# Weights split in place, and two staging tiles for every bank, in a two-block transformer kernel

## What is computed

```
h = rms_norm(x, norm_mix)
(a_q, a_kc, ..., merge_gate) = split(h @ w_in)
x = x + sum(sigmoid(merge_gate) * (branches @ w_branch)) @ w_out
x = x + square(relu(rms_norm(x, norm_mlp) @ w_mlp_in)) @ w_mlp_out
...
mod = silu(c) @ w_mod[l] + b_mod[l]
u = h @ e_w_in;  x = x + gate * (y @ w_o[l])
```

## Time and profile before

| | |
|---|---|
| median of 3 runs | 3655.73 us |
| the profiled execution | 3658.32 us |
| its span | 3656.5 us |
| mean granted TensorE clock | 0.947 of full speed |
| PE busy | 3305.0 us (90%), 15207 matmuls |
| DVE busy | 1742.6 us (48%) |
| ACT busy | 1489.2 us (41%) |
| low parts, L394 | 986 of mean 1210 ns |
| high parts, L388 | 986 of mean 1044 ns |
| evacuations to staging, L465 | 148 of 128 partitions and 20 of 4 |
| weight loads from SP | median 4.4 to 7.1 us from issue to landing, by matrix |

### The profile page before, as it was taken

How to read it: one execution, slowest core, us unless ns; L and a number is a source line. 1 busy time by engine, 2 the same in 40 slices (tenths; PEclk the granted TensorE clock), 3 DMA queues, 4 the chain that set the end, 5 groups by cost and what they waited for, 6 DMA issues and landing times.

```text
span 3656.5 us, 39374 instructions
## 1 busy us (share of the span) xinstructions
PE 3305.0 (90%) x15207; PEld 2656.6 (73%) x15207; DVE 1742.6 (48%) x2450; ACT 1489.2 (41%) x2230; POOL 230.2 (6%) x351
## 2 busy tenths in 40 slices
PE   5999999799899999999969999999975979787867
PEld 4888888677778788888847877777754868665546
DVE  3445555455565655666553233334333353345534
ACT  3444444333454554545553232333332143243532
POOL 0000000010000000000010000000011000010010
PEclk9999999899899999999979999999986979898978
DMA  7666745465577777877653423223333215544653
GB/s 216 221 215 226 254 127 182 158 213 184 188 251 236 249 250 241 276 237 254 230 157 102 136 76 113 96 97 114 107 134 120 93 55 157 166 156 148 203 176 124
DMA packets 355878, 634.40 MB, mean 173 GB/s; under 512 B 44715, under 2 KB 111944, under 8 KB 352620
## 3 DMA queue, kind: packets, MB, share of 16 engines
q1 hardware_dynamic: 319772, 543.49, 45.8%
q0 software_dynamic: 19936, 69.22, 5.3%
q10 hardware_dynamic: 15984, 19.17, 1.6%
HBM read 583.00 MB, written 55.08 MB: 175 GB/s over the span
## 4 chain that ended last, share of the span: by engine, by line
PE 81%; DVE 6%; ACT 4%; issue 3%; DMA 3%; POOL 1%; ACTq 1%; SPq 0%; DVEq 0%; POOLq 0%
PE acc L413 24%; PE acc L418 21%; PE acc L417 21%; PE acc L987 3%; PE acc L1014 3%; PE acc L415 2%; DVE w_lo L394 2%; PE acc L1002 2%; PE acc L645 1%; ACT w_hi L388 1%; ACT aff L679 1%; PE acc L991 1%; PE acc L971 1%; ACTq L1145 1%; ACT xn L760 0%
## 5 line engine op out<-in xcount | busy, mean ns | idle before, releaser
L413 PE MATMUL acc<-w_hi,a_hi 128*128 128x512 f32 (+4 forms) x3800 | 1509.1, 397 | 65.0 <-issue 24.1
L394 DVE TENSOR_TENSOR w_lo<-raw,w_hi 128x1024 fp32r<-128x1024 f32 (+1 forms) x986 | 1159.8, 1210 | 840.0 <-ACT w_hi L388 822.6
L417 PE MATMUL acc<-w_lo,a_hi 128*128 128x512 f32 (+4 forms) x3800 | 1474.8, 388 | 0.0
L418 PE MATMUL acc<-w_hi,a_lo 128*128 128x512 f32 (+4 forms) x3800 | 1474.2, 388 | 0.0
L388 ACT ACTIVATE w_hi<-raw 128x1024 fp32r<-128x1024 f32 (+1 forms) x986 | 1000.1, 1044 | 892.6 <-PE acc L418 881.6
L413 PEld LDWEIGHTS acc<-w_hi,a_hi 128*128 128x128 f32 x3800 | 720.9, 190 | 230.8 <-DVE w_lo L394 43.1
L418 PEld LDWEIGHTS acc<-w_hi,a_lo 128*128 128x128 f32 x3800 | 720.3, 190 | 146.9
L417 PEld LDWEIGHTS acc<-w_lo,a_hi 128*128 128x128 f32 x3800 | 721.0, 190 | 132.6 <-issue 1.0
L1111 DVE TENSOR_REDUCE at_st<-acc 128x1 f32<-128x256 f32 (+3 forms) x208 | 101.3, 487 | 445.4 <-PE acc L987 302.3
L1044 ACT ACTIVATE pb<-acc,at_st 128x256 f32<-128x256 f32 (+3 forms) x208 | 108.5, 521 | 381.5 <-DVE at_st L1111 358.3
L645 PE MATMUL acc<-ident,xn 128*128 128x128 f32 x336 | 86.7, 426 | 161.4 <-DVE xn L1688 49.0
(11 more groups left out here) (316 smaller groups left out, 1659.5 us busy)
## 6 DMA issues: line engine op xcount, KB each, us to landing
raw<-in_w_mod SPq DMA_DIRECT2D x192, 512.0 KB, 5.2
raw<-in_w_mlp_in SPq DMA_DIRECT2D x128, 512.0 KB, 4.6
raw<-in_w_mlp_out SPq DMA_DIRECT2D x128, 512.0 KB, 5.4
raw<-in_e_w_in SPq DMA_DIRECT2D x104, 512.0 KB, 5.0
raw<-in_w_in SPq DMA_DIRECT2D x96, 512.0 KB, 4.8
raw<-in_w_in SPq DMA_DIRECT2D x88, 472.0 KB, 4.8
raw<-in_w_o SPq DMA_DIRECT2D x64, 512.0 KB, 4.9
raw<-in_o_w_in SPq DMA_DIRECT2D x64, 512.0 KB, 4.4
```

What stands on the lines that cost most here:

```text
L394: nc.vector.tensor_tensor(w_lo[:, n % SPLITS, 0:size], raw[:, n % RAWS, 0:size], w_hi[:, n % SPLITS, 0:size].bitcast(F32), ALU.subtract)\
L413: nc.tensor.matmul(o, s.lhs(0, kt, tt), wh, start=kt == 0, stop=False)
L417: nc.tensor.matmul(o, s.lhs(0, kt, tt), wl, start=False, stop=False)
L418: last = nc.tensor.matmul(o, s.lhs(1, kt, tt), wh, start=False, stop=end)
```

## The change

The low part of a chunk is written over the raw chunk that it comes from: `w_lo` is placed at the address of `raw`, with 8 tiles in place of 4, and DVE's instruction at L394 writes where it reads. A raw tile is therefore in use until PE has done the chunk's last matmul, and SP waits for `w_used` of chunk n - 8 where it waited for `lo_ready` of chunk n - 8. The four tiles of `w_lo` (16 KB in each partition) are gone. In their room every bank gets a second staging tile (8 KB more for the four banks, 2 KB more for bank 4), used in turn by the bank's count of stores `put`; each of the two has a semaphore of its own, so that ACT waits for the bank's store before the last one. `put_by` replaces the waits of the readers of stored results: it waits on both semaphores of a bank.

```diff
--- before.py
+++ after.py
@@ -138,9 +138,9 @@
             return nc.dram_tensor(name, shape, F32, kind="Internal").ap()
 
 
-        raw = sb("raw", [P, RAWS, CH])
+        raw_at = take(4 * RAWS * CH)
+        raw, w_lo = place("raw", [P, RAWS, CH], raw_at), place("w_lo", [P, RAWS, CH], raw_at, F32R)
         w_hi = sb("w_hi", [P, SPLITS, CH], F32R)
-        w_lo = sb("w_lo", [P, SPLITS, CH], F32R)
         act_hi_at, act_lo_at = take(32768), take(32768)
         a_hi = place("a_hi", [P, 8192], act_hi_at, F32R)
         a_lo = place("a_lo", [P, 8192], act_lo_at, F32R)
@@ -148,7 +148,7 @@
         CX_AT = take(16384)
         CX = place("CX", [P, 2, DM], CX_AT)
         MIX = CX
-        stage = sb("stage", [P, 4, G])
+        stage = sb("stage", [P, 8, G])
         ident = sb("ident", [P, P])
         small = sb("small", [P, 64])
         half = sb("half", [P, 2])
@@ -338,8 +338,12 @@
         w_used = sem("w_used")
         acc_done = [sem(f"acc_done{b}") for b in range(3)]
         acc_free = [sem(f"acc_free{b}") for b in range(5)]
-        stored = [sem(f"stored{b}") for b in range(5)]
-        stage_bufs = [stage[:, b, :] for b in range(4)] + [sb("stage_mod", [4, G])[:, :]]
+        stored = [[sem(f"stored{b}_{i}") for i in range(2)] for b in range(5)]
+        stage_mod = sb("stage_mod", [4, 2, G])
+
+        def stage_buf(bank, put):
+            return stage_mod[:, put % 2, :] if bank == 4 else stage[:, 2 * bank + put % 2, :]
+
         nsa_g = sb("nsa_g", [P, 2, 24])
         nsa_ready, nsa_out = sem("nsa_ready"), sem("nsa_out")
         mfr, mfb, mfo = sb("mfr", [P, 4, NM]), sb("mfb", [P, NM]), sb("mfo", [P, 2, NM])
@@ -371,7 +375,7 @@
         def sp_chunk(sp, g, c):
             n = g.no[c]
             if n >= RAWS:
-                sp.wait_ge(lo_ready, n - RAWS + 1)
+                sp.wait_ge(w_used, n - RAWS + 1)
             dst = raw[:, n % RAWS, 0:g.wtiles * g.width].rearrange("p (k n) -> p k n", k=g.wtiles)
             sp.dma_start(dst, g.chunks[c]).then_inc(landed[n % RAWS], 16)
 
@@ -391,7 +395,7 @@
         def split_lo(dve, s, c):
             n, size = s.no[c], s.wtiles * s.width
             dve.wait_ge(hi_ready, n + 1)
-            nc.vector.tensor_tensor(w_lo[:, n % SPLITS, 0:size], raw[:, n % RAWS, 0:size],
+            nc.vector.tensor_tensor(w_lo[:, n % RAWS, 0:size], raw[:, n % RAWS, 0:size],
                                     w_hi[:, n % SPLITS, 0:size].bitcast(F32), ALU.subtract)\
               .then_inc(lo_ready, 1)
 
@@ -408,7 +412,7 @@
                 o = acc[:, bank, 0:s.width]
                 kt = c * s.wtiles + k
                 wh = w_hi[:, n % SPLITS, k * s.width:(k + 1) * s.width]
-                wl = w_lo[:, n % SPLITS, k * s.width:(k + 1) * s.width]
+                wl = w_lo[:, n % RAWS, k * s.width:(k + 1) * s.width]
                 end = kt == len(s.chunks) * s.wtiles - 1
                 nc.tensor.matmul(o, s.lhs(0, kt, tt), wh, start=kt == 0, stop=False)
                 if s.lhs is lhs_mod:
@@ -455,14 +459,14 @@
             for bank, tt in s.tiles:
                 if e["kind"] == "store":
                     wait_done(act, s, bank)
-                    if s.put[bank]:
-                        act.wait_ge(stored[bank], 16 * s.put[bank])
+                    if s.put[bank] >= 2:
+                        act.wait_ge(stored[bank][s.put[bank] % 2], 16 * (s.put[bank] // 2))
                     r = e["rows"]
                     if e.get("gates"):
                         c0 = e["gates"]
                         nc.scalar.activation(nsa_g[:, tt, :], acc[:, bank, c0:c0 + 24], ACT.Tanh, scale=0.5)\
                           .then_inc(nsa_ready, 1)
-                    nc.scalar.activation(stage_bufs[bank][0:r, 0:s.width], acc[0:r, bank, 0:s.width],
+                    nc.scalar.activation(stage_buf(bank, s.put[bank])[0:r, 0:s.width], acc[0:r, bank, 0:s.width],
                                          e["func"], scale=e["scale"]).then_inc(acc_free[bank], 1)
                 elif e["kind"] == "relu2":
                     wait_done(act, s, bank)
@@ -550,8 +554,8 @@
             e = s.evac
             for bank, tt in s.tiles:
                 pool.wait_ge(acc_free[bank], s.fill[bank] + 1)
-                pool.dma_start(e["dst"](tt, s.width), stage_bufs[bank][0:e["rows"], 0:s.width])\
-                    .then_inc(stored[bank], 16)
+                pool.dma_start(e["dst"](tt, s.width), stage_buf(bank, s.put[bank])[0:e["rows"], 0:s.width])\
+                    .then_inc(stored[bank][s.put[bank] % 2], 16)
             if e.get("gates"):
                 pool.wait_ge(nsa_ready, 2)
                 pool.dma_start(AG.rearrange("(t p) n -> p t n", p=P), nsa_g[:, :, :]).then_inc(nsa_out, 16)
@@ -576,18 +580,23 @@
                 elif s.evac["kind"] == "store":
                     pool_store(pool, s)
 
+        def put_by(eng, bank, k):
+
+            for i in range(2):
+                if (k + 1 - i) // 2:
+                    eng.wait_ge(stored[bank][i], 16 * ((k + 1 - i) // 2))
+
         def wait_stored(eng, upto):
 
             for b in range(5):
                 k = stages[upto].upto.get(("put", b), 0)
-                if k:
-                    eng.wait_ge(stored[b], 16 * k)
+                put_by(eng, b, k)
 
         def wait_step(eng, name, i):
 
             s_ = stages[name].steps[i]
             for bank, _ in s_.tiles:
-                eng.wait_ge(stored[bank], 16 * (s_.put[bank] + 1))
+                put_by(eng, bank, s_.put[bank] + 1)
 
         def wait_freed(eng, upto):
```

## The result

| kernel | median us | runs | lowest to highest |
|---|---|---|---|
| before | 3656.95 | 17 | 3649.93 to 3658.91 |
| after | 3664.95 | 17 | 3661.13 to 3670.70 |

The ratio is 1.0024, 95% interval 1.0017 to 1.0032: slower by 0.24%, outside the range of 3649 to 3662 and on the side that had 8%. The profiled execution took 3664.08 us, its span 3662.3, 5.8 more than the span before. Two of all executions, one of e4 (4147 us, granted clock 0.77) and one of the kernel before beside e5 to e8 (4922 us, 0.65), ran at a lower clock than the rest and stand in no median.

What follows compares the result with a forecast made beforehand. The prediction took PE's weight matmuls (PE busy 90%) as the bound. Staging tile -1.1 and small waits +0.2, all else 0, gave -0.9 us: 3657.4 for the profiled execution, 3654.8 against the median, range 3649 to 3662.

Steps and rivals of the forecast that it cites:

- SP's later wait: Weight loads wait for PE's last use, going out up to four chunks later: 0 us, bounds 0 and +3.7.
- What stands behind SP's later wait: Attention pass rows on SP's in-order queue come some 11 us later, but are read 30 or 86 us on: 0.
- opening: Weight loads at 49 to 93 us: shorter queue, chunk 15 still 0.9 us in time; 0, upper bound 2.6.
- compression weights: Loads at 350 to 370 us: 7.5 us to land against a slowest 7.6, just in time; 0, bound +0.2.
- MLP: MLP with modulation steps beside it: 11.0 us left for landing against a slowest 7.3; covered.
- The first rival: Opening starves PE, landings keeping 18.8 us: 3660.9, or 3664.5 with PE at half clock after stalls; chance 7%.
- any pass starts later than its predecessor's end moved: One of the prediction's own tests, over all passes: if seen, the forecast is wrong.
- Second staging tile: ACT's waits for QB and KVB stores go, saving PE 0.45 and 0.65 us: -1.1, bounds 0 and -11.3.
- The second rival: ACT's staging waits in the attention passes are worth all their 11.3 us: 3644.6; chance 5%.
- the third: Staging evacuations stay late, so the change does nothing and only +0.2 stands: 3655.9; chance 4%.
- Low parts in place: DVE's subtraction writing over its input takes no longer: 0, at most 1.9 us on the path either way.
- Small waits: Readers of stores on SP, POOL and ACT wait on two semaphores instead of one: +0.2, bounds 0 and +1.

Runs made afterwards that it cites:

- e4: Kernel before, with SP's rows for the third attention region's first pass held until PE's last use of chunk 879; 3660.40 us.
- e5: Changed kernel, third region's first rows moved after its fifth chunk, loads from chunk 705 held until the modulation vector landed; 3657.48 us.
- e8: Kernel before, with the third region's first rows moved and holds at chunks 705, 815 and 888; 3649.88 us.
- e7: Kernel before, with SP's late wait for PE's matmuls at chunks 704 to 712 only; 3659.26 us.
- e1: Kernel before, with only SP's wait changed, to PE's last use of chunk n - 8; 3668.85 us.
- e9: Changed kernel, with the third region's first rows moved and holds at chunks 215, 705, 815 and 886; 3648.61 us.
- e10: e9 with only the first staging tile of each bank in use; 3650.88 us.
- e11: Kernel before, with SP's late wait at all chunks plus e9's holds and moved rows; 3654.69 us.
- e3: Changed kernel, with the third attention region's first rows and loads issued behind its fifth weight chunk instead of ahead of its first; 3661.25 us.
- e6: e5 with two more holds, at chunk 815 for the second modulation vector and chunk 888 for the low-rank norms' loads; 3654.26 us.

## Why the prediction was wrong

**SP's later wait: 0, bounds 0 and +3.7.** The step that failed is the paragraph "What stands behind SP's later wait". It took the rows at 3139.93, found their first reader 86 us on the earlier trace rows, and wrote "I take 0 for all". The 0 counts only who waits for the moved transfer, not whose transfer it then runs beside. The reader's slack was right: nobody waited for them. But a transfer costs others too. What I had to ask of every moved DMA is which small transfer with a waiter it now runs beside. The cost measured, alone: +3.6 (e4, this place; 3.9 in its step), +2.1 (e7, the MLP's end; 2.7 in its step, and its interval includes 0). With the less certain one at 808 it is 7.6 us of steps in the changed kernel, and the late wait as a whole cost 12 in e1.

The sign was in the rows. The prediction put PE's 27.0 us of waits for low parts at step starts, "and the change leaves that order alone". 14.6 of them are the single wait at 3180.28, for the norms' chain of store, loads and DVE: the one that grew to 19.7.

I also looked for trouble only where the queue was slow in reaching PE: opening, compression weights, MLP. There I was right. In the opening, 54 to 92 us, the loads land after

```profile
DMA to landing us min/median/max: 4.7/10.2/12.4
```

in place of 11.9/16.2/18.8, as I wrote (8 to 13) but for the quickest, and PE needs 102.02 us from the end of chunk 1 to that of chunk 40 in both kernels. The line in the queue was a line, and it got shorter. The first rival named the right side, slower, for the wrong reason: by it PE would have starved there. Its 3664.5 is near the time measured, which proves nothing for it. Nor does the half clock that it takes from the gap at 3247 follow from that gap: in before the granted clock was already 0.50 from 3240 on, in an idle of 9.08 us that ended at 3243.

Of my own tests the nearest was "any pass starts later than its predecessor's end moved"; what it caught is not a pass but the norms ahead of one, at DVE's first multiply.

**Second staging tile: -1.1, bounds 0 and -11.3.** Right in kind and place, half of what came in size: -2.3 in e9 against e10, and -2.2 in the step 885 to 900 of the changed kernel. The evacuation that had waited at 3216.76 no longer waits for a store; PE passes without the gap of the earlier trace rows. At the two places of the sum the changed kernel gains 0.54 (chunk 894, 0.45 forecast) and 0.84 us (chunk 900, 0.65 forecast); the other 0.8 of its 2.2 lies at chunks 886 and 888, ahead of any QB evacuation, and isn't the tile's. In e9 against e10 the gain is spread over chunks 894 to 900. The second rival, the full 11.3, is excluded by the same pair, and so is the third, that it does nothing.

**Low parts in place: 0, bound 1.9 either way.** The instruction's time was right: 1210 ns mean after as before. The term was not, as far as the pair e10 and e11 measures it alone: 3.8 us gained, twice the bound, with no place for it.

**Small waits: +0.2.** No run separates them; too small to be measured.

In sum: -0.9 was forecast and +8.0 came. The later wait had 0 in it where e1 shows +12; the staging tile and the low parts give back about 2 and 3 to 4. 12 less 5 to 6 is 6 to 7 where 8.0 was measured; the rest is within what these medians can tell: they and the traces differ by as much (8.0 between medians, 5.8 between spans).

## What to carry to other kernels

When a change moves bulk loads later, their readers' slack is half the question. List the small stores and loads that some engine waits for (a result to DRAM and back, a vector, a gain row) and look at what the bulk queue now does in those microseconds. An early prefetch is worth something by having got out of the way. And where such a chain is on the path, hold the bulk loads for it: with tiles full ahead of it no cost of the hold shows here (chunks 704 to 720 take 87.04 us and 808 to 820 65.28 us in every trace, held or not), and four holds and a moved block of rows turned +8.0 into -8.2 us. Try the holds on the kernel before as well: there three of them and the rows gave -7.3 without the change, and a comparison with the held change alone would have credited the change with it.

## What the runs showed that I had not expected

A store of 8 KB landed in about 1.8 us beside a nearly idle queue, and in 3.4 to 4.0 us beside weight loads; the last of four stores of 160 KB in 2.06 and in 3.8 to 5.6. Separate queues do not keep a small transfer from a large one's company. The Trainium skill, "DMA: Bandwidth & Descriptors", section "Latency and other measured facts", puts the time to DRAM at 0.2 us on average and 2 us at high load. The 1.7 to 2.2 us more at the 8 KB store are of that size; no run separates that from taking turns.

TensorE's clock can differ after one and the same idle. Before and after both have PE waiting 2.22 us for ACT's copy `pt` near 2587 us; then the clock is (window, PE busy, granted clock, DMA share, GB/s) in before and in after

```profile
2588.00:2592.00 4.00, 4.00 (x22) 1.00 0.00 0
```

```profile
2588.00:2592.00 4.00, 4.00 (x17) 0.57 0.00 0
```

1.00 is the level of 2.4 GHz, and 0.57 is mostly that of 1.2 GHz. It costs 1.6 us: over the 13 traces the step to chunk 792 is 13.9 or 15.4 us, the step to 800 is 11.9 or 13.5, and neither goes with any edit (e7 has the long one at 792 and the short one at 800, e6 the other way). The step to chunk 753 varies more, from 7.7 to 13.0 us, and PE waits for `pt` in it too. In before it waits 2.02 us, goes on at the full clock and takes 9.64 us for the step; in e3 it waits 1.89 us and the granted clock is 0.85 over the step (11.09 us), in e1 2.54 us and 0.74 (13.04 us). Nothing that e3 changed comes before it (8.42 us in after). So 3.4 of e1's 12 us may be this and not the small transfers; no run settles it. One pair of traces can't tell such a jump from an effect of 1.5 us; a dozen can.
